# Rebuilt seams, four-part first loads and constant matmuls in the idle stretches of a ten-stage network kernel

## What is computed

```python
def rms_norm(x, g):
    xf = x.astype(jnp.float32)
    return xf * lax.rsqrt(jnp.mean(xf * xf, -1, keepdims=True) + EPS) * g.astype(jnp.float32)

x = x + mix.astype(x.dtype)
h = rms_norm(x, norm_ffn_g[layer]).astype(x.dtype)
x = x + conv_ffn(h, ...)
```

```python
h = swiglu(rms_norm_2(x, ffn1_norm_pre[l]), ffn1_w_gate[l], ffn1_w_up[l], ffn1_w_down[l])
x = x + 0.5 * rms_norm_2(h, ffn1_norm_post[l])
h = hybrid_mixer(rms_norm_2(x, mix_norm_pre[l]), ...)
x = x + rms_norm_2(h, mix_norm_post[l])
h = swiglu(rms_norm_2(x, ffn2_norm_pre[l]), ffn2_w_gate[l], ffn2_w_up[l], ffn2_w_down[l])
x = x + 0.5 * rms_norm_2(h, ffn2_norm_post[l])
```

## Time and profile before

| | us |
|---|---|
| median of three runs | 3544.43 (3542.8 to 3549.26) |
| the profiled execution, its own time | 3546.43 |
| its span from first to last instruction | 3544.7 |
| TensorE (PE) busy in matmuls | 3306.8 |
| DVE, ACT, POOL busy | 1220.6, 1171.5, 1439.7 |

### The profile page before, as it was taken

How to read it: one execution, slowest core, us unless ns; L and a number is a source line. 1 busy time by engine, 2 the same in 40 slices (tenths; PEclk the granted TensorE clock), 3 DMA queues, 4 the chain that set the end, 5 groups by cost and what they waited for, 6 DMA issues and landing times.

```text
span 3544.7 us, 38416 instructions
## 1 busy us (share of the span) xinstructions
PE 3306.8 (93%) x15164; PEld 2683.6 (76%) x15164; DVE 1220.6 (34%) x1586; ACT 1171.5 (33%) x1208; POOL 1439.7 (41%) x1112
## 2 busy tenths in 40 slices
PE   7869999988899999999799989998999899989997
PEld 5638888867688888888587868886888677868885
DVE  6244332132543312220645442204221364642212
ACT  3344442242243323322324343223332233433321
POOL 4204444522155544445351244453444363044443
PEclk9959999998899999999899999998999899999998
DMA  3102223311122232222221122232222232022222
GB/s 137 71 0 83 95 95 107 111 60 60 36 95 95 95 107 96 100 101 104 87 105 47 48 71 95 95 107 72 95 95 107 80 120 84 1 72 96 101 100 83
DMA packets 44916, 301.84 MB, mean 85 GB/s; under 512 B 5248, under 2 KB 7552, under 8 KB 9104
## 3 DMA queue, kind: packets, MB, share of 16 engines
q1 hardware_dynamic: 40176, 292.79, 23.2%
q10 hardware_dynamic: 4640, 7.57, 0.7%
HBM read 296.15 MB, written 2.10 MB: 84 GB/s over the span
## 4 chain that ended last, share of the span: by engine, by line
PE 88%; DVE 7%; issue 3%; ACT 2%; DMA 0%; DVEq 0%; ACTq 0%; SPq 0%
PE main L431 77%; PE misc L1502 2%; PE main L1611 1%; PE main L1468 1%; PE misc L450 1%; PE misc L1484 1%; DVE rstd L585 1%; PE main L1413 1%; DVE x L684 1%; DVE y L679 1%; PE main L1472 1%; DVE acc L593 0%; PE main L1118 0%; DVE od_state L1308 0%; DMA stage<-in_w 0%
## 5 line engine op out<-in xcount | busy, mean ns | idle before, releaser
L2073 POOL TENSOR_TENSOR w_lo<-stage,w_hi 128x512 fp32r<-128x512 f32 x1108 | 1439.5, 1332 | 2069.4 <-ACT w_hi L490 2069.4
L431 PE MATMUL main<-h_hi,w_lo 128*128 128x512 f32 x2840 | 1126.1, 397 | 86.7 <-DVE h_lo L693 60.5
L431 PE MATMUL main<-h_lo,w_hi 128*128 128x512 f32 x2840 | 1113.9, 392 | 0.0
L431 PE MATMUL main<-h_hi,w_hi 128*128 128x512 f32 x2840 | 1113.8, 392 | 0.0
L431 PEld LDWEIGHTS main<-h_hi,w_lo 128*128 128x128 f32 x2840 | 539.4, 190 | 217.1 <-issue 97.6
L490 ACT ACTIVATE w_hi<-stage 128x2048 fp32r<-128x2048 f32 x277 | 527.8, 1911 | 426.7 <-DMA stage<-in_w 415.1
L431 PEld LDWEIGHTS main<-h_lo,w_hi 128*128 128x128 f32 x2840 | 539.6, 190 | 116.0 <-issue 4.8
L431 PEld LDWEIGHTS main<-h_hi,w_hi 128*128 128x128 f32 x2840 | 538.4, 190 | 113.6
L431 PE MATMUL main<-hid_hi,w_lo 128*128 128x512 f32 x1248 | 486.7, 390 | 0.2 <-DVE hid_lo L1329 0.2
L431 PE MATMUL main<-hid_lo,w_hi 128*128 128x512 f32 x1248 | 485.8, 389 | 0.0
L431 PE MATMUL main<-hid_hi,w_hi 128*128 128x512 f32 x1248 | 485.6, 389 | 0.0
(11 more groups left out here) (311 smaller groups left out, 2507.1 us busy)
## 6 DMA issues: line engine op xcount, KB each, us to landing
stage<-in_w SPq DMA_DIRECT2D x277, 1024.0 KB, 4.8
x<-in_xT SPq DMA_DIRECT2D x1, 2048.0 KB, 8.0
out_x<-x ACTq DMA_DIRECT2D x1, 2048.0 KB, 6.4
b_r<-sq ACTq DMA_DIRECT2D x4, 256.0 KB, 8.3
b_r<-sq ACTq DMA_DIRECT2D x4, 255.5 KB, 9.1
ev_ws<-in_ev_ws ACTq DMA_DIRECT2D x1, 512.0 KB, 4.2
b_pos<-in_pos ACTq DMA_DIRECT2D x2, 256.0 KB, 3.9
b_cmask<-in_b_cmask ACTq DMA_DIRECT2D x2, 256.0 KB, 4.7
```

The costliest lines, as they stand in the source:

```text
L431: last = pe.matmul(acc[:, m, :], w[a], r[b], start=start and k == 0 and j == 0, stop=stop and k == nk - 1 and j == 2)
L2073: last = e.tensor_tensor(c.w_lo[:, s, k:k + 2, :].rearrange("p k n -> p (k n)"), c.stage[:, s, k * CW:(k + 2) * CW], c.w_hi[:, s, k:k + 2, ...
```

## The change

- **Sums of squares.** `token_sums` takes the four 128-token pieces of the summed squares as the stationary operand and one column of ones as the moving one: the sums stand in four columns, tokens on the partitions. Root and reciprocal work on 128x4. `norm_diag` makes four diagonal tiles of them, and `spread` multiplies ones by these, which gives the 128x512 factor in m[1]. For a pre-norm `norm_copy` copies it to `rstd`; in a post-norm DVE reads it in PSUM. `join_banks` adds the two halves of `acc`.
- **Pre-norm sums move into the products** of the second chunk (`norm_hooks`: `sum_squares` at k=1, `spread` at k=3), in an FFN into the last k of the first pair and k=1 of the third chunk.
- **Post-norm.** ACT squares each PSUM bank of a result directly, DVE takes it out with the gain on it. The last group's chunk is done half by half (`chunk_halves`), so that its first bank's squares are summed (`first_sums`) before the last products end. The table of the root is loaded ahead. x and h advance one tile at a time instead of two.
- **FFN.** The first two chunks are done together, k by k (`first_pair`), the second into two `misc` banks (`extra_slot`); later slots turn accordingly (`Count.slot`). The split of a chunk in a pair moves behind `hid_hi`.
- **NSA.** The first chunk does its `h_hi` products before it waits for `h_lo` (`first_chunk`), and `turn_k` and `turn_v` stand behind the fourth chunk instead of the third.
- **Start.** x and the first weight chunk come in four parts each, in turn. **End.** The store is in four parts.
- **Constant matmuls.** `keep_busy` puts products of `ident` and `ones` into m[3]: 5 and 9 in each post-norm, 20 ahead of the first chunk.

The core of the diff:

```diff
+def token_sums(pe, c, src, start, stop):
+    for i in range(TT):
+        last = pe.matmul(c.m[0][:, i:i + 1], src[:, i * P:(i + 1) * P], c.ones[:, 0:1],
+                         start=start and i == 0, stop=stop and i == TT - 1)
+    return last
 def sum_squares(pe, n, c):
-    n.skip(c.acc_ready, 4)
+    n.skip(c.acc_ready, 5)
     pe.wait_ge(c.acc_ready, n(c.acc_ready))
-    for j in range(2):
-        last = pe.matmul(c.m[0][:, :], c.ones[:, :], c.acc[:, j, :], start=j == 0, stop=j == 1)
-    last.then_inc(c.ssq_ready, 1)
+    token_sums(pe, c, c.acc[:, 0, :], True, True).then_inc(c.ssq_ready, 1)
+def spread(pe, n, c):
+    for i in range(TT):
+        pe.wait_ge(c.diag_ready, n(c.diag_ready))
+        last = pe.matmul(c.m[1][:, i * P:(i + 1) * P], c.ones[:, :], c.diag[:, i, :], start=True, stop=True)
+    last.then_inc(c.spread_ready, 1)
+def norm_hooks(pe, n, c):
+    return {1: lambda: sum_squares(pe, n, c), 3: lambda: spread(pe, n, c)}
+def first_pair(pe, n, c, accs):
+    slots = [n.chunk % RING, (n.chunk + 1) % RING]
+    pe.wait_ge(c.w_lo_done, n(c.w_lo_done, 2))
+    for k in range(KT):
+        if k == KT - 1:
+            sum_squares(pe, n, c)
+        pe.wait_ge(c.h_hi_done, n(c.h_hi_done))
+        for j in range(2):
+            for m in range(2):
+                w = (c.w_hi[:, slots[j], k, m * P:(m + 1) * P], c.w_lo[:, slots[j], k, m * P:(m + 1) * P])
+                pe.matmul(accs[j][:, m, :], w[1], c.h_hi[:, k, :], start=k == 0, stop=False)
+                pe.matmul(accs[j][:, m, :], w[0], c.h_hi[:, k, :], start=False, stop=False)
+        pe.wait_ge(c.h_lo_done, n(c.h_lo_done))
...
+def keep_busy(pe, c, k):
+    for _ in range(k):
+        pe.matmul(c.m[3][:, 0:P], c.ident[:, :], c.ones[:, :], start=True, stop=True)
+def first_sums(pe, n, c):
+    pe.wait_ge(c.p_total, n(c.p_total))
+    token_sums(pe, c, c.acc[:, 0, :], True, False)
+def last_sums(pe, n, c):
+    pe.wait_ge(c.p_sqb, n(c.p_sqb, 4))
+    token_sums(pe, c, c.sq[:, 1, :], False, True).then_inc(c.ssq_ready, 1)
+    keep_busy(pe, c, 5)
+    spread(pe, n, c)
+    keep_busy(pe, c, 9)
...
 def ffn_in_scalar(act, n, c, conv):
     def pair(e, i, last=False):
-        split_next(e, n, c)
...
+        if not last:
+            split_next(e, n, c)
     split_next(act, n, c)
-    norm_std(act, n, c)
+    split_next(act, n, c)
+    norm_copy(act, n, c)
...
+    for k in range(KT):
+        dve.tensor_tensor(c.y[:, k, :], c.y[:, k, :], c.m[1][:, :], ALU.mult).then_inc(c.post_y, 1)
+        dve.wait_ge(c.post_y, n(c.post_y))
+        dve.tensor_tensor(c.x[:, k, :], c.x[:, k, :], c.y[:, k, :], ALU.add).then_inc(c.x_ready, 1)
...
+        if k >= 1:
+            low(k - 1)
+        if k in (5, 7):
+            gather_squares(dve, n, c, k // 2 - 1)
+    low(7)
+    gather_squares(dve, n, c, 3)
+    join_banks(dve, n, c)
...
 even_tensor:
+    n.skip(c.h_hi_done, KT)
+    keep_busy(pe, c, 20)
     z(pe, wait_k=c.h_lo_done)
-    sum_squares(pe, n, c)
-    for j in range(4):
+    z(pe, at=norm_hooks(pe, n, c))
+    head_norm()
+    for j in range(3):
...
 nsa_tensor:
-    z(wait_k=c.h_lo_done)
-    z(mid=lambda: sum_squares(pe, n, c))
+    first_chunk(pe, n, c, group_slot(pe, n, c))
+    chunk_products(pe, n, c, group_slot(pe, n, c), c.h_hi, c.h_lo, KT, at=norm_hooks(pe, n, c))
+    z()
     z()
     pe.wait_ge(c.turn_loaded, 16 * (l + 1))
     turn_k()
     turn_v()
     z()
     z()
-    z()
...
-            sp.dma_start(c.x[:, :, :], a["xT"]).then_inc(c.x_loaded, 16)
+            for p in range(PARTS):
+                sp.dma_start(two(c.x, p), a["xT"][:, 2 * p:2 * p + 2, :]).then_inc(c.x_part[p], 16)
+                sp.dma_start(c.stage[:, 0, p * PART:(p + 1) * PART], first[:, p * PART:(p + 1) * PART])\
+                    .then_inc(c.w_part[p], 16)
...
-    act.wait_ge(c.last_ready, 1)
-    act.dma_start(out, c.x[:, :, :]).then_inc(c.stored, 16)
-    act.wait_ge(c.stored, 16)
+    for m in range(4):
+        act.wait_ge(c.last_ready, m + 1)
+        act.dma_start(out[:, 2 * m:2 * m + 2, :], two(c.x, m)).then_inc(c.stored, 16)
+    act.wait_ge(c.stored, 64)
```

More of the change, by code:

```diff
@@ new lines, in norm_hooks @@
+def norm_hooks(pe, n, c):
[13 more added lines that the diff above has]
+        pe.wait_ge(c.h_lo_done, n(c.h_lo_done))
+        for j in range(2):
+            for m in range(2):
+                last = pe.matmul(accs[j][:, m, :], c.w_hi[:, slots[j], k, m * P:(m + 1) * P], c.h_lo[:, k, :],
+                                 start=False, stop=k == KT - 1)
+            if k == KT - 1:
+                last.then_inc(c.chunk_done, 1)
+    n.chunk += 2
@@ new lines, in first_chunk @@
+def first_chunk(pe, n, c, acc):
+    s = n.chunk % RING
+    pe.wait_ge(c.w_lo_done, n(c.w_lo_done))
+    for k in range(KT):
+        pe.wait_ge(c.h_hi_done, n(c.h_hi_done))
+        for m in range(2):
+            w = (c.w_hi[:, s, k, m * P:(m + 1) * P], c.w_lo[:, s, k, m * P:(m + 1) * P])
+            pe.matmul(acc[:, m, :], w[1], c.h_hi[:, k, :], start=k == 0, stop=False)
+            pe.matmul(acc[:, m, :], w[0], c.h_hi[:, k, :], start=False, stop=False)
+        pe.wait_ge(c.h_lo_done, n(c.h_lo_done))
+        for m in range(2):
+            last = pe.matmul(acc[:, m, :], c.w_hi[:, s, k, m * P:(m + 1) * P], c.h_lo[:, k, :],
+                             start=False, stop=k == KT - 1)
+    last.then_inc(c.chunk_done, 1)
+    n.chunk += 1
@@ new lines, in chunk_halves @@
+def chunk_halves(pe, n, c, acc, hi, lo, nk, k0, start, mid):
+    s = n.chunk % RING
+    pe.wait_ge(c.w_lo_done, n(c.w_lo_done))
+    for m in range(2):
+        for k in range(nk):
+            if m == 1 and k == nk - 2:
+                mid()
+            w = (c.w_hi[:, s, k, m * P:(m + 1) * P], c.w_lo[:, s, k, m * P:(m + 1) * P])
+            r = (hi[:, k0 + k, :], lo[:, k0 + k, :])
+            for j, (a, b) in enumerate(((1, 0), (0, 1), (0, 0))):
+                last = pe.matmul(acc[:, m, :], w[a], r[b], start=start and k == 0 and j == 0,
+                                 stop=k == nk - 1 and j == 2)
+        last.then_inc((c.bank0_done, c.chunk_done)[m], 1)
+    n.chunk += 1
@@ L669, in result_vector @@
-    n.loop(dve, 2, lambda e, i: (one(e, 2 * i), one(e, 2 * i + 1)))
-    n.skip(c.acc_ready)
-    if post is not None:
-        norm_recip(dve, n, c)
-        if norm is not None:
-            clear_squares(dve, n, c)
-        rstd = over_tiles(c.rstd[:, :])
-        for m in range(6 if norm is not None else 5):
+    if post is None:
+        clear_squares(dve, n, c)
+        for m in range(4):
+            n.skip(c.chunk_done, chunks - 1)
+            dve.wait_ge(c.chunk_done, n(c.chunk_done))
+            acc = c.ps[n.slot()]
+            n.group += 1
+            dve.tensor_tensor(two(c.x, m), acc[:, :, :], two(c.x, m), ALU.add).then_inc(c.group_taken, 1)
+            dve.wait_ge(c.group_taken, n(c.group_taken))
+            next_h_vector(dve, n, c, m, norm)
+        join_banks(dve, n, c)
+        return
@@ L1613, in half @@
         return last
+    c.result_slot[post] = n.slot()
     slots = [n.chunk % RING, (n.chunk + 1) % RING]
```

363 lines of the change are left out of this document (234 added, 129 removed).

## The result

The changed kernel takes 3494.82 us (median of 4 runs, 3489.74 to 3498.61), the kernel before, beside it, 3545.39 (4 runs, 3542.8 to 3549.26). The ratio is 0.9856, with a 95% interval of 0.9838 to 0.9873. The time lies inside the range on record (3456 to 3502), but outside the forecast's own part of it (3458 to 3484); the size of 72.9 does not hold. The profiled execution has a span of 3494.6 against 3544.7.

The account below looks back on a forecast made before the run. The prediction took the serial chain over DVE, ACT and PE in the seams as the bound. Gains of 42.3+11.8+0+9.9+8.9 = 72.9 us gave 3471.5 us, own range 3458 to 3484, widened over rivals to 3456 to 3502.

Parts of the forecast that it names:

- the range on record: Forecast for the whole kernel: 3456 to 3502 us, reaching over the clock rival and the lower edge of the new wait.
- the size of 72.9: Whole kernel: total forecast gain in us, the sum 42.3+11.8+0+9.9+8.9.
- the clock rival: Rival, chance 0.22: the clock is not held in the seams, constants take twice; about 22 us less gain, 3493 us.
- The seam into an FFN: Three post-norm seams: first product at T+6.25 instead of T+20.25; 14.1 us gained each, 42.3 in all.
- T: Start of the last matmul of a stage, from which the prediction counts its times.
- the wait of 1.4: FFN seam, third chunk: PE loses 1.4 us because w_lo is ready only at T+30.7.
- The seam into the NSA mixer: Two post-norm seams: fifth chunk starts at T+66.1 instead of T+72.9; 5.9 us gained each, 11.8 in all.
- a new wait eats the seams: Rival, chance 0.13: w_lo, diagonals behind ACT's issues or DVE with POOL cost 5 to 8 us more per seam.
- Pre-norm seams at zero: Four pre-norm seams: PE has no gap there, so no gain, between -1 and +1 us each.
- Tail: Kernel end: end near T+17.9 instead of 28.65 us; gain 10.75, net 9.9 after 0.87 ahead of T.
- Start: First loads: `ones` lands at 9 us, second chunk ends earlier; gain 8.9 us, range 5.7 to 11.4.
- The 11.4 us: Start's larger gain: smaller parts on SP's queue let ACT's tables through sooner, with `ones` landing at 6.5 us.

Follow-up runs that it names:

- Experiment 2: Changed kernel with turn_k and turn_v put back behind the third chunk in the NSA mixer: 3474.26 us, ratio 0.9798 to the kernel before.
- experiment 4: Changed kernel with turns back behind the third chunk, and root and split ahead of the memory wait and table loads: 3466.87 us, ratio 0.9778 to the kernel before.
- Experiment 3: Changed kernel with ACT's root and split ahead of the memory wait and seven table loads in the NSA mixer: 3483.79 us, ratio 0.9829 to the kernel before.
- experiment 5: Changed kernel without the 5 and 9 constant matmuls of each post-norm, those at the start kept: 3504.21 us, ratio 0.9889 to the kernel before.
- the better one: Changed kernel with both NSA order edits: 3471.46 us without any constant matmuls, 3463.84 us without only those at the start.
- experiment 8: Changed kernel with 10 and 18 constant matmuls in each post-norm instead of 5 and 9: 3509.53 us, ratio 0.9902 to the kernel before.
- experiment 7: Changed kernel with x and the first weight chunk as one transfer each instead of four parts: 3497.34 us, ratio 0.9874 to the kernel before.
- 9: Changed kernel with both NSA order edits, the code of experiment 4 run again: 3470.1 us, ratio 0.9794 to the kernel before.
- experiment 6: Changed kernel without the 20 constant matmuls at the start, those of the seams kept: 3496.26 us, ratio 0.9866 to the kernel before.

## Why the prediction was right in sign and too large in size

**How the number came to lie in the range.** The forecast's own range, 3458 to 3484, missed; the range on record was widened over two rivals, and 3494.8 lies in that part. It lies next to the 3493 of the clock rival, whose state did not occur. That is luck: the time went in the NSA seams, in a step that the forecast had priced wrongly and in new waits.

**The seam into an FFN: right, by its own steps.** First product at T+6.60 for 6.25; the third chunk's split at T+21.7 for 23.65; `acc` done at T+25.5 for 25.65; four diagonals in the post-norm took 0.88, where 0.28 each had been taken. The token sums at k=7 stand at T+25.8. The third chunk's `w_lo` was ready at T+29.2 and not T+30.7, since ACT's split came 2 us earlier, so the wait of 1.4 did not appear. The four diagonals at T+27.3 took 4.46 us beside POOL's eight `w_lo` pieces for 0.88 without them, but PE stood 0.16 us for them only, as it had the rest of the pair and the first six products of the third chunk to do meanwhile. The spread ends at T+32.3 for 31.6, with these six products (1.37 us) already done; like for like that is 0.7 better than forecast. 43.0 came of 42.3. (Two sums of the prediction are off by half a us: its prices from T+4.05 on give `acc` at T+25.2, not T+25.65, and its four prices behind the fourth chunk give T+65.6, not T+66.1. Neither decides anything.)

**The seam into the NSA mixer: the failed step.** The prediction says: "`turn_k` now stands behind the fourth: its product 0.86, rope multiply, rope add and the `b_u` take (0.69, 0.7, 1.22) give the fifth chunk its bank at +66.1." It followed `turn_k` into DVE and left out that `turn_v` moves with it and feeds ACT. From the fourth chunk's end to the fifth's start, 4.0 us were forecast; it took 10.8 (1761.95 to 1772.72): products 1.3, `b_va` 0.6, split 1.8, `b_a_hi` 0.9, `b_a_lo` 1.4, then the rotation and `b_u`. Before, the same row of ACT work hung on DVE's angle work and let `b_a_lo` start at 1765.59, T+66.8; now it hangs on the fourth chunk, and `b_a_lo` starts at T+71.3. Experiment 2 undoes that order alone, takes 10.1 and 10.5 us off the two stretches, and the two seams gain 4.8 and 7.6 on the kernel before. The step is shown. That this is 6.2 in the mean where 5.9 each was forecast is a coincidence: it still holds the second loss, and with that gone too (experiment 4) the seams gain 8.4 and 11.0.

The second part is the other 4.5 of the 11.2 us by which the fifth chunk is late on its forecast: the second chunk ended at T+44.7, not T+40.2. The root came at T+30.6, a little earlier than T+31.8, and PE's wait for the first diagonal, put at 3.1, was 3.65. What was not foreseen came behind it. The other three diagonals stood beside POOL and took 3.75 us in the chain, where 0.28 each had been taken, so that the spread lasted 4.5 us instead of 0.87; and the 30 products behind it took 8.1 us instead of 6.8, with the clock down in part (0.85 from 1719 to 1732). This is the rival "a new wait eats the seams" in its place, "the diagonals behind ACT's issues, or DVE paired with POOL". Experiment 3 removes all of it, the foreseen wait too, and gives 6.7 and 7.1. It moves the diagonals out from under POOL and the root out from behind the issues in one edit; by the rows, some 3.7 us is the wait behind the issues and the rest is POOL and the clock, but no run takes them apart.

**The clock rival: right about what is at stake, wrong about what happens.** The constants hold the clock: 1.00 through the seam with them, 0.50 behind it without them (experiment 5). The prediction's 22 us were for constants that are there and don't hold the clock, a state that no run shows in a seam. Leaving them out costs 8 us in the changed kernel by the medians (9.6 by the stretches) and 7.6 in the better one (5 by the stretches, less firmly). Five and nine are enough; doubled, they cost 13 us (experiment 8).

**Pre-norm seams at zero: right, as far as can be told.** The first stretch kept 3.45 of the 6.9 us gained at its start. The odd mixer alone, from its first product of `h_hi` to its first of `hid_hi`, takes 257.0 us in the trace of before and 260.2 in that of the changed kernel. But the same code takes 257.5 in four of the twelve traces behind the change (experiments 2, 3, 7 and 9) and 260.0 to 260.2 in the other eight, and PE's wait for `od_vs`, 21.5 us above, goes with it. In experiment 2 it is what it was before:

```profile
PE misc L1321 <- DVE od_vs L1503: 15.9, 4, 4.4
```

So at most 0.5 of the 3.2 us belongs to the change. The even mixer behind its second chunk varies as well, from 218.1 to 224.4 us (222.5 before). From the odd mixer's first product of `hid_hi` to the first T all twelve traces have 767.9 to 768.0, before it was 766.7: 1.3 longer, 0.87 of it `first_sums`. Why these two mixers have more than one length, no run here tells.

**Tail: 11.9 for 10.75.** The end came at T+16.8 instead of T+17.9. DVE was done at T+13.4 for 14.0, and the last store took 3.3 of the 3.9 left for it; a part of 512 KB lands in 2.7 us in the median, where the nearest row had 4.2.

**Start: 6.9 for 8.9 (6.2 in the mean of eight traces): near, by a step that does not hold.** `ones` landed at 9.55 where 9 was taken and the first product came at 16.40; 40 records took 7.09 for 6.7. But the prediction lets the end of the second chunk follow the first product at a fixed distance of 23.6 us, and it does not: in experiment 6 the first product came 5.0 us earlier and the second chunk ended 0.9 earlier (1.6 against the mean of eight). What stands in the chain there is DVE, eight pieces of `h_lo` and the additions to `acc`. So the closeness is in part luck. The Trainium skill ("DMA: Bandwidth & Descriptors", "Queues, rings and completion order") has a DMA engine go round its queues a packet at a time. The traces agree in the direction: with parts SP's packets are smaller (2.7 KB in the mean against 7.8) and `ones`, on ACT's queue, lands at 7.58 to 9.55 instead of 12.23 (experiment 7). The 11.4 us that the prediction drew from it did not come, for the reason just given.

## What to carry to other kernels

When a piece of work is moved on one engine's queue, follow every consumer of it on every other queue, and what is queued behind that consumer: here the loss came not from the value that was moved but from its neighbour, whose copy stood ahead of an unrelated operation that a third engine needed. Measure stages from marker to marker and not from the start of the span; fixed stretches show an effect of 2 us where the medians barely show 8, once several traces of the same code have shown how firm each stretch is. Constants that keep the clock up are worth something only in a gap that really idles PE, and no more of them than fill it.

## What the runs showed of the hardware

- The clock fell behind idle pieces of 0.96 and 2.35 us with 8 short matmuls between them, and was down for the next 12 full products (experiment 5). The Trainium skill ("TensorE: Matmul & The Clock Gate", "Part 1: The HAM clock gate") has the low clock as the default that activity releases; the runs agree in the seams, where constants held it. At the start no run shows them to help: seven of nine traces with 20 more matmuls under the loads show a lower clock for some 3 us around 30 us, none of the three without.
- DVE beside POOL: four 128x128 diagonals took 0.88 us with POOL idle and 4.46 with POOL in its `w_lo` pieces. Of the 64 diagonals of the changed kernel's trace, the 40 with POOL idle took 0.27 to 0.29 us each, the 24 beside POOL 0.73 to 1.34, up to the length of one of POOL's pieces (1.3 us).
- A one-column fp32 matmul costs no less than one of 65 columns: 8 records in 0.80 us in the chain of the changed kernel, 0.10 each, against 0.108.
- Transfers in smaller parts had smaller packets and let a 64 KB table on another queue land 2.7 to 4.7 us earlier (12.23 against 7.58 to 9.55).
